# Low weight parts of the first block's branch and output projections, made half by GpSimd and half by VectorE

## The reference

```python
z = h @ p['w_in'] + p['b_in']
y_hy = hyena(z[..., COL_HY:COL_Q], p) @ p['w_hy_out']            # (256, 512) @ (512, 1024)
y_na = attend(q, k, v).reshape(B, L, D_NA) @ p['w_na_out']       # (256, 512) @ (512, 1024)
gate = jax.nn.sigmoid(z[..., COL_G_HY:N_PROJ])
merged = gate[..., :D_MODEL] * y_hy + gate[..., D_MODEL:] * y_na
return merged @ p['w_out']                                       # (256, 1024) @ (1024, 1024)
```

## Time and profile before

| | |
|---|---|
| time, median of 3 runs | 2204.08 us (2203.77 to 2205.78) |
| span of the profiled execution | 2202.9 us |
| PE busy | 1984.4 us (90%) |
| VectorE busy | 1357.5 us (62%) |
| ACT busy | 1011.5 us (46%) |
| GpSimd busy | 1039.6 us (47%) |
| stage of the change | from 297 to 369 us |

### The profile page before, as it was taken

One profiled execution on the slowest core, in us unless ns is written; L12 is line 12 of the kernel. 1 busy time (PEld: TensorE's weight loads), 2 busy tenths in 40 slices (PEclk: granted clock), 3 DMA queues, 4 the chain that ended last, 5 costly groups with the idle time before them and its releaser, 6 DMA issues.

```text
span 2202.9 us, 27135 instructions
## 1 busy us (share of the span) xinstructions
PE 1984.4 (90%) x9640; PEld 1470.3 (67%) x9640; DVE 1357.5 (62%) x2766; ACT 1011.5 (46%) x1852; POOL 1039.6 (47%) x840
## 2 busy tenths in 40 slices
PE   7999987887877878778999999989999999998998
PEld 1777766833333333333599777889989977778998
DVE  3767855586666676665367753267754775426776
ACT  1623545422212122221545687455564568845555
POOL 2362576754344443443587666800038865781000
PEclk9999999999899888999999999999999999999999
DMA  9132765699999999999555444545545534454553
GB/s 354 66 139 81 258 231 181 253 422 422 421 421 422 421 421 422 421 421 422 211 178 168 139 160 152 185 150 183 191 155 178 191 125 154 163 181 155 191 181 114
DMA packets 111449, 534.40 MB, mean 243 GB/s; under 512 B 12497, under 2 KB 12881, under 8 KB 77905
## 3 DMA queue, kind: packets, MB, share of 16 engines
q1 hardware_dynamic: 67104, 244.72, 32.6%
q0 software_dynamic: 38720, 275.96, 30.4%
q10 hardware_dynamic: 5488, 11.98, 1.6%
HBM read 531.49 MB, written 1.11 MB: 242 GB/s over the span
## 4 chain that ended last, share of the span: by engine, by line
PE 60%; DMA 22%; ACT 7%; DVE 5%; issue 3%; POOL 2%; ACTq 0%; DVEq 0%; SPq 0%; POOLq 0%
PE psum L881 59%; DMA pair_rows<-in_peer_uv,arena 9%; DMA arena<-in_peer_uv,arena 8%; DMA wring<-in_peer_uv,arena 4%; ACT w_hi L1446 2%; PE psum L949 2%; POOL w_lo L2828 1%; ACT arena L1457 1%; POOL w_lo L2826 1%; DVE arena L1980 1%; DMA wring<-in_w_ada 1%; ACT arena L1800 1%; ACT a_hi L1453 0%; ACT arena L1671 0%; ACT arena L1818 0%
## 5 line engine op out<-in xcount | busy, mean ns | idle before, releaser
L2826 POOL TENSOR_TENSOR w_lo<-wring,w_hi 128x512 fp32r<-128x512 f32 x280 | 375.8, 1342 | 544.0 <-ACT w_hi L1446 533.5
L1446 ACT ACTIVATE w_hi<-wring 128x1024 fp32r<-128x1024 f32 (+1 forms) x414 | 433.5, 1053 | 331.9 <-PE psum L881 280.8
L881 PE MATMUL psum<-w_hi,a_hi 128*128 128x512 f32 (+1 forms) x1056 | 423.1, 401 | 21.7 <-POOL w_lo L2828 12.1
L881 PE MATMUL psum<-w_lo,a_hi 128*128 128x512 f32 (+1 forms) x1056 | 411.2, 389 | 0.0
L881 PE MATMUL psum<-w_hi,a_lo 128*128 128x512 f32 (+1 forms) x1056 | 410.7, 389 | 0.0
L881 PE MATMUL psum<-arena 128*128 128x512 f32 (+7 forms) x1142 | 338.5, 453 | 68.5 <-ACT arena L1671 50.6
L2828 POOL TENSOR_TENSOR w_lo<-wring,w_hi 128x512 fp32r<-128x512 f32 x280 | 393.0, 1404 | 0.0
L881 PE MATMUL psum<-a_hi,w_hi 128*128 128x256 f32 x1312 | 379.1, 289 | 10.7 <-DVE a_lo L1975 8.7
L881 PE MATMUL psum<-a_lo,w_hi 128*128 128x256 f32 x1312 | 374.2, 285 | 0.0
L881 PE MATMUL psum<-a_hi,w_lo 128*128 128x256 f32 x1312 | 374.1, 285 | 0.0
L881 PEld LDWEIGHTS psum<-arena 128*128 128x128 f32 (+2 forms) x1142 | 185.8, 198 | 201.2 <-issue 121.9
(11 more groups left out here) (261 smaller groups left out, 2379.8 us busy)
## 6 DMA issues: line engine op xcount, KB each, us to landing
wring<-in_w_up SPq DMA_DIRECT2D x88, 512.0 KB, 3.4
wring<-in_w_xbc SPq DMA_DIRECT2D x48, 512.0 KB, 3.3
wring<-in_w_dn SPq DMA_DIRECT2D x44, 512.0 KB, 3.3
wring<-in_w_adaT SPq DMA_DIRECT2D x32, 512.0 KB, 4.3
wring<-in_w_qkv SPq DMA_DIRECT2D x32, 512.0 KB, 3.6
wring<-in_w_z SPq DMA_DIRECT2D x32, 512.0 KB, 3.3
wring<-in_w_g SPq DMA_DIRECT2D x32, 512.0 KB, 3.3
wring<-in_w_ps SPq DMA_DIRECT2D x32, 512.0 KB, 3.3
```

The source lines that it names most:

```text
L881: mm = lambda o, a, b, start, stop: nc.tensor.matmul(o, a, b, start=start, stop=stop, skip_group_check=True)
L1446: a.reaches(A(w_hi[:, n % SPLIT_RING, 0:width], wring[:, c % RING, 0:width], ACT.Copy), hi_ready, n + 1)
L2826: nc.gpsimd.tensor_tensor(w_lo[:, r, 0:half], wring[:, c % RING, 0:half], w_hi[:, r, 0:half].bitcast(F32), ALU.subtract)
```

## The change

For the sixteen chunks of `w_hy_out`, `w_na_out` and `w_out`, GpSimd makes columns 0 to 511 of `w_lo` and VectorE columns 512 to 1023. `low_cols` holds for each chunk which engine makes which columns, and the count of its semaphore. TensorE and SP wait for both counts (`wait_low`). VectorE's halves are placed by its own `SplitStream`, and before each dot `weights_behind` places the halves of all chunks whose ring place has been loaded anew by then, since the dot's chunk is loaded only behind them.

```diff
+    low_cols, low_counts = {}, {"pool": 0, "vector": 0}
     for n_, c_ in enumerate(split_chunks):
+        name_, width_ = wplan[c_][0], wplan[c_][3]
+        by_vector = width_ if name_ in ("w2_up", "w2_dn") or 0 <= c_ - second_block < 2 else 0
+        if name_ in ("w_hy_out", "w_na_out", "w_out"):
+            by_vector = width_ // 2
+        for who, cols_ in (("pool", (0, width_ - by_vector)), ("vector", (width_ - by_vector, width_))):
+            if cols_[0] < cols_[1]:
+                low_counts[who] += 1
+                low_cols[(n_, who)] = (cols_, low_counts[who])
+
+    def wait_low(eng, n):
+
+        if (n, "pool") in low_cols:
+            eng.wait_ge(lo_ready, low_cols[(n, "pool")][1])
+        if (n, "vector") in low_cols:
+            eng.wait_ge(lo_ready_v, low_cols[(n, "vector")][1])
...
                 if c - RING in split_turn:
-                    sp.wait_ge(*low_done(split_turn[c - RING]))
+                    wait_low(sp, split_turn[c - RING])
...
             n, width = split_turn[c], wplan[c][3]
-            pe.wait_ge(*low_done(n))
+            wait_low(pe, n)
...
+            (at, end), r = low_cols[(n, "vector")][0], n % SPLIT_RING
...
+            v.reaches(T.tensor_tensor(w_lo[:, r, at:end], wring[:, c % RING, at:end], w_hi[:, r, at:end].bitcast(F32),
+                                      ALU.subtract), lo_ready_v, low_cols[(n, "vector")][1])
...
+        def weights_behind(c):
+            loaded = [f for f in split_chunks if f <= c - RING]
+            if loaded:
+                streams[id(dve)].upto(loaded[-1])
+
         def ada_dots(n0, n1):
             dve.wait_ge(S("c_row_ready"), 1)
             for n in range(n0, n1):
                 c = ada_chunks[n]
                 w = wring[:, c % RING, :]
+                weights_behind(c)
                 dve.wait_ge(weights_in[c % RING], 16 * (c // RING + 1))
...
+            if width < wplan[c][3]:
+                nc.gpsimd.tensor_tensor(w_lo[:, r, 0:width], wring[:, c % RING, 0:width],
+                                        w_hi[:, r, 0:width].bitcast(F32), ALU.subtract).then_inc(lo_ready, 1)
+                return
```

More of the change, by code:

```diff
@@ L537, in build @@
     lo_ready_v = S("weights_lo_ready_vector")
-    low_turn, low_counts = {}, {"pool": 0, "vector": 0}
+    low_cols, low_counts = {}, {"pool": 0, "vector": 0}
     for n_, c_ in enumerate(split_chunks):
[L540 to L547, removed]
+        name_, width_ = wplan[c_][0], wplan[c_][3]
[11 more added lines that the diff above has]
+            eng.wait_ge(lo_ready_v, low_cols[(n, "vector")][1])
     dot_turn = {c: n for n, c in enumerate(c for c, w in enumerate(wplan) if w[0] == "w_adaT")}
@@ L1888, in weights_low @@
         def weights_low(n, c):
-            if low_turn[n][0] != "vector":
+            if (n, "vector") not in low_cols:
                 return
             dve.wait_ge(hi_ready, n + 1)
-            width, r = wplan[c][3], n % SPLIT_RING
+            (at, end), r = low_cols[(n, "vector")][0], n % SPLIT_RING
             if c >= second_block and c < second_block + 2:
                 dve.wait_ge(S("pair_used"), split_freed((SPLIT_RING + r) * CHUNK))
-            v.reaches(T.tensor_tensor(w_lo[:, r, 0:width], wring[:, c % RING, 0:width], w_hi[:, r, 0:width].bitcast(F32),
-                                      ALU.subtract), *low_done(n))
+            v.reaches(T.tensor_tensor(w_lo[:, r, at:end], wring[:, c % RING, at:end], w_hi[:, r, at:end].bitcast(F32),
+                                      ALU.subtract), lo_ready_v, low_cols[(n, "vector")][1])
         streams[id(dve)] = SplitStream(weights_low)
@@ L2815, in weights_low @@
         def weights_low(n, c):
-            if low_turn[n][0] != "pool":
+            if (n, "pool") not in low_cols:
                 return
             pool.wait_ge(hi_ready, n + 1)
-            width, r = wplan[c][3], n % SPLIT_RING
+            width, r = low_cols[(n, "pool")][0][1], n % SPLIT_RING
             if c == chunk_at[("w_pq", None, 1)]:
@@ L2862, in _ @@
                 weights_upto(pool, "w_pq", None, ring_chunk(RING_PLACES[n - 4]) - last_query + 15)
-                pool.wait_ge(*low_done(split_turn[ring_chunk(RING_PLACES[n - 4])]))
+                wait_low(pool, split_turn[ring_chunk(RING_PLACES[n - 4])])
             if n == 7:
```

## The result

The changed kernel took 2210.63 us in the median of 9 runs (2208.76 to 2215.07), the kernel before 2204.08 (2202.77 to 2206.84): a ratio of 1.0029, with a 95% interval from 1.0021 to 1.0038. It is slower by 6.5 us, or 0.3%, more than the 0.2% that the prediction took for what a measurement of this kernel can tell. The forecast was 2204.8 and no change, with a range up to 2210.0. It was wrong: the loss was foreseen at 0.7 us and as no change that could be told, and the time lies 0.6 us above the range.

The account below looks back on a forecast made before the run. TensorE's pace was taken to bound most of the kernel, with waits for GpSimd and VectorE in turn in this stage. Terms -0.3, +3.0, +0.5 and -2.5 made +0.7 on 2204.08: 2204.8 us, range 2199.5 to 2210.0.

Parts of the forecast that it names:

- Step 1: At hy0, both halves end near 299.8, so TensorE starts at 299.9 and not 300.62: 0.7 us won.
- Step 2: Behind hy0, the shorter wait removes the low clock stretch: 1.7 us more, a head start of 2.4 us.
- Step 3: At hy3, VectorE's half stands behind three dots and GpSimd's turns: 2.8 us lost, 0.4 net of time won earlier.
- Step 4: At na0, D27 is loaded later, over hy3, so na0 starts 1.2 us late, net of time won earlier.
- Step 5: Dot D29 starts between 328.0 and 330.7 against 329.69; taken as 0.3 us early.
- Step 6: From D29 to out0 on VectorE, five added halves and GpSimd's turns, less waits saved at sums: +3.0 us.
- Step 7: At out0, TensorE's wait grows to some 4 us; low stretch already there, 0.5 us allowed for a second.
- Step 8: At out4 to out7, chunks come in turns of 1.7 us and TensorE's waits go: 2.5 us won.
- three signs: Wrong if hy3 starts under 3 us after hy2's end, out0 comes 5 us after 339.08, or out6 still waits 2 us.
- B: Rival, slower: VectorE's chain from D29 to out0 replaces the waits for GpSimd; 2210.3 us (2209.5 to 2211.2), 17%.
- A: Rival, faster: VectorE's halves are never late, so TensorE's waits for GpSimd go but for 1.6 at hy0; 2197.4 us, 12%.
- C: Rival: VectorE and GpSimd don't take turns, so hy3's half and all behind come 3.2 us earlier; 2201.6 us, 8%.

Follow-up runs that it names:

- before_fourth: The kernel before, unchanged, run once for one more profile: 2203.98 us.
- no_middle: The changed kernel, but na3 and out0 to out3 are GpSimd's alone as before: 2207.42 us, ratio 1.0014 to the kernel before.
- tail_only: The changed kernel, but only out4 to out7 are made in halves, the other twelve chunks by GpSimd alone: 2202.33 us, ratio 0.9994 to the kernel before.
- delay_2us: The kernel before plus eleven tiny VectorE instructions, about 2.1 us, ahead of the low parts of mT: 2206.79 us, ratio 1.0012.
- middle_only: The kernel before with only na3 and out0 to out3 made in halves: 2207.31 us, ratio 1.0012.
- hy3_first: The changed kernel with VectorE's half of hy3 ahead of the dots D24 to D26: 2207.89 us, ratio 1.0022 to the kernel before.
- combined: The kernel before with hy0 to hy2 and out4 to out7 halved, hy3 whole on VectorE ahead of its dots: 2197.84 us, again 2199.85 (ratios 0.9970, 0.9980).

## Why the prediction was wrong, point by point

**Step 1, hy0: right in the start.** 299.9 was said, 299.71 came. The wait was 0.79 us and not 1.6, since TensorE was there at 298.9 and not at 298.3.

**Step 2, the clock behind hy0: wrong, and the first cause of the miss.** In the trace of the change the low stretch was gone as forecast, and hy2 started 2.5 us earlier than in the first profile (2.4 said). But I booked 1.7 us of that as won by the change. The kernel before runs the same products in 7.1 us in three of four traces. The wait of 2.22 us in before_fourth had no low stretch behind it either, so its length, by which I took the stretch as gone, does not decide here. The low stretch belonged to the one execution that I read. Without it the head start is 0.7 us, and that case had been worked out: +2.4 us.

**Step 3, hy3: right in mechanism, the clock missing.** The order of turns came as written: D25, GpSimd's half of na0, D26, GpSimd's of na1, then the half of hy3 with 1.74 us. The start was 315.94 (318.4 - 2.4 = 316.0 said) and the wait 6.04. What I left out is that the low clock goes with the longer wait: it falls on hy3 in all six traces of the changed kernel and in that of no_middle, all with a wait of 6.0 us. Of the seven traces with a wait of 3.2 us there (the four of before, tail_only, delay_2us and middle_only) it falls on hy3 in two. That the wait causes it is argued from this alone. I had priced the low stretch at hy3 as there already, by the earlier trace rows, which is that one trace.

**Step 4, na0: right.** A wait of 0.8 us was said, 1.09 came, and D27's load was issued at 315.87.

**Step 5, D29: within its ends.** 330.24, where 328.0 to 330.7 stood and 329.4 was taken: 0.8 us too early. VectorE was free for it at 328.6, and its load ended the wait.

**Step 6, from D29 to out0: right.** 12.4 us said, 12.45 measured (330.24 to 342.69). The half of out3 took 1.75 us in turn with GpSimd. The sums got part of their time back: three of the four took 0.69 and one 1.08. In the means of all traces the stretch took 9.9 us before and 12.8 after, so this step holds against them too: +2.9, and 3.0 was said.

**Step 7, the clock at out0: the same error as in 2.** The low stretch there was taken as present in the kernel before. It is there in full in one trace of four, and in all six after: 1.1 us in the mean (8.9 against 7.8), where I had 0.5 for a second one.

**Step 8, out4 to out7: too good by 1.0 us.** out0 to out6 took 20.96 us and not 22.47, so 1.5 are won and not 2.5. The clock is low in its first part in both. The wait before out6 is 0.90, where I had none: the half of out7 stands behind both updates of `x`, which themselves stand behind three halves that took 5.2 us in turns.

```profile
355.01 5.22 DVE L1903 TENSOR_TENSOR w_lo<-wring,w_hi 128x512 fp32r<-128x512 f32 x3 [2.85 <-ACT w_hi L1453]
...
362.82 0.68 DVE L1903 TENSOR_TENSOR w_lo<-wring,w_hi 128x512 fp32r<-128x512 f32 x1
```

That was in my own terms, and I added it up wrongly. From 356.4, where I had the half of out6 end, four operations of 0.69 and a half of 0.6 lead to 359.8 and not to the 358.7 that stood there: 0.8 us behind TensorE's 359.0.

Against the profile of before out6 came 2.1 us later (361.55 to 363.65), where the sum said 0.2 before the allowance of step 7: the differences of steps 5 and 8. Against the mean of four executions of the kernel before the stage lost 4.0 us (69.7 to 73.7). By the means of the traces, counted from the stage's start:

| | said | measured |
|---|---|---|
| up to D29 (steps 1 to 5) | -0.3 | +1.5 |
| D29 to out0 (step 6) | +3.0 | +2.9 |
| out0 to out6 (steps 7 and 8) | -2.0 | -0.4 |
| sum | +0.7 | +4.0 |

So the steps that failed are 2 and 7, where one execution's low stretches were booked as won or as there already, and 5 and 8, each some 0.8 to 1.0 us too good. Of the 3.3 us missed in the stage, 2.5 are the base (the first profile's 72.2 against 69.7), and not all of that is the clock: D29's load is in it too.

None of the three signs that I had set for a wrong forecast came: hy3 started 6.0 us behind hy2, out0 3.6 us later than 339.08, and out6 waited 0.9. All three were set against the one profile, and so they could not show that it was the wrong base.

**Behind the stage** I had said that it is passed on whole. delay_2us bears that out within its interval. In the traces the changed kernel loses another 0.8 us at the queries, which I had at nothing, and the second block is 1.9 us shorter, for which no run gives a cause.

**The rivals.** B had the right place in part (the chain on VectorE) and with 2209.5 to 2211.2 the right time, with 17%. That is luck for its number: its condition was not met. Only two GpSimd halves fell between D29 and out0 (332.56 and 339.28), D29's load took 6.2 us and not 6.8, and step 6 came out at 3.0 and not 5.2. A fell: the halves were late. C fell: the engines did take turns in each place looked at.

**What stays open.** The traces show 3.0 us between the means of the two kernels from the stage's start on (1896.7 and 1899.7 us to the last product). The times say more. The changed kernel's six profiled executions took 2207.3 us in the mean, and the 22 others 2211.1; for the kernel before the three profiled ones with a time took 2203.9 and 19 others 2202.9. So about half of the 6.5 us is in executions of the changed kernel that left no trace. To be profiled does not make an execution fast: those of hy3_first and no_middle were the slowest of their kernels. Each execution's mean granted clock is known, and it points at the clock: 0.9622 in the 22 of the changed kernel without a trace, 0.9643 in its six with one, and 0.9649 in the 19 of the kernel before. From 0.9643 to 0.9622 is about 9 us more at the low level in 2209, which by my estimate costs up to half of that, and the difference is 3.8. Where in the program these stretches lie, and whether the change brings them, no run here tells.

## What to carry to other kernels

Work that is handed to an idle engine is done when its place in that engine's order comes, not when its input is there: count what stands ahead of it, and where two engines take turns, the other one's instruction for each. Halving a task between two engines that take turns shortens it only by the difference of their speeds. Giving hy3 whole to the faster one, ahead of its other work and where it stood idle, gained some 2 us; a kernel with only hy3 halved at that place was not run, so the two are not compared directly. And never book a low clock stretch of a single execution as something that a change wins back, or as cover for one that it brings: take a second profile of the kernel before, which showed 2.3 us less in this stage.

## What the runs showed of the hardware that was not expected

A kernel's stage of 70 us, with the same instructions in the same order, took from 67.9 to 72.2 us in four executions. Low stretches under products at hy0 and at out0 make 1.6 us each of that, and D29's load, with 5.7 to 7.8 us from issue to dot, a part of the rest. Yet the changed kernel with its 6 us wait gave 73.2 to 74.1 in six: with the long wait the low stretch came each time.

VectorE's low part of 128 x 1024 took 1.22 us beside no GpSimd work (combined), and GpSimd's two halves of the same 2.5 alone and 4.3 (311.26 to 315.56) in turns with two dots. Taking turns was seen for the pairs that were looked at: dots 2.11 to 2.31 against 1.23, halves 1.74 and 1.75 against 0.68. VectorE's products that read PSUM and one SBUF tile kept their 0.68 beside GpSimd's low parts of 1.71 us (332.53 and 334.21 in the first profile).
